# A decoder layer on one core: its first stage in pairs of token tiles

## What is computed

```
mod = silu(c) @ w_ada + b_ada                       # six rows of 1024: shift_a, scale_a, gate_a, ...
h   = rms_norm(x, g_attn) * (1 + scale_a) + shift_a # rms_norm: x * rsqrt(mean(x*x) + eps) * g
proj = h @ w_in                                     # queries, latents, index keys, keys, values
```

## Time and profile before

| | |
|---|---|
| median of 3 runs | 1016.02 us (1015.51 to 1017.2) |
| the profiled execution, its own time | 1018.29 us |
| its span in the profile | 1016.4 us |
| PE busy | 946.8 us, 93% of the span |
| DVE busy | 593.9 us, 58% |
| ACT busy | 401.1 us, 39% |
| POOL busy | 117.9 us, 12% |
| mean granted clock of PE, as a share of full speed | 0.971 |

### The profile page before, as it was taken

One profiled execution on the slowest core, in us unless ns is written; L12 is line 12 of the kernel. 1 busy time (PEld: TensorE's weight loads), 2 busy tenths in 40 slices (PEclk: granted clock), 3 DMA queues, 4 the chain that ended last, 5 costly groups with the idle time before them and its releaser, 6 DMA issues.

```text
span 1016.4 us, 14951 instructions
## 1 busy us (share of the span) xinstructions
PE 946.8 (93%) x5302; PEld 514.1 (51%) x5302; DVE 593.9 (58%) x1593; ACT 401.1 (39%) x909; POOL 117.9 (12%) x218
## 2 busy tenths in 40 slices
PE   3899999999999999999999999996699999979975
PEld 3464575444448756777766455554233433323421
DVE  2388647999999699987777234366222333212217
ACT  6131235666650488777668121212111221111113
POOL 3001000000008411110000000000111111111003
PEclk9999999999999899999999999998799999989988
DMA  9997100110111000040000421198799999999979
GB/s 325 331 358 266 42 22 23 41 42 23 41 42 27 1 1 2 1 182 9 1 2 1 186 83 63 66 368 325 278 404 421 420 420 420 419 422 420 394 291 373
DMA packets 70956, 191.96 MB, mean 189 GB/s; under 512 B 10264, under 2 KB 37200, under 8 KB 58592
## 3 DMA queue, kind: packets, MB, share of 16 engines
q1 hardware_dynamic: 62896, 173.15, 44.7%
q0 software_dynamic: 5760, 16.78, 4.2%
q10 hardware_dynamic: 2224, 1.05, 0.4%
HBM read 173.12 MB, written 22.04 MB: 192 GB/s over the span
## 4 chain that ended last, share of the span: by engine, by line
PE 65%; DVE 21%; DMA 6%; issue 5%; ACT 1%; POOL 1%; SPq 0%; POOLq 0%; DVEq 0%; ACTq 0%
PE PS L2006 12%; PE PS L1891 11%; DVE BIAS L1157 8%; PE PS L1784 6%; PE PS L2029 5%; PE PS L1827 5%; PE PS L1849 4%; DMA SC<-in_w_up_dram 3%; PE PS L1745 3%; PE PS L1697 3%; PE PS L1844 2%; DMA X<-residual_rows 2%; DVE X L1221 2%; PE PS L1993 2%; PE PS L1722 2%
## 5 line engine op out<-in xcount | busy, mean ns | idle before, releaser
L1697 PE MATMUL PS<-HT,X 128*128 128x512 f32 x384 | 168.8, 593 | 0.0
L2006 PE MATMUL PS<-QKV,HT 128*32 128x512 f32 (+2 forms) x640 | 131.2, 611 | 3.3 <-ACT HT L966 1.7
L870 ACT ACTIVATE X<-X,nmx 128x128 f32<-128x128 f32 (+7 forms) x128 | 98.4, 770 | 54.4 <-DVE nmx L1221 54.1
L1697 PEld LDWEIGHTS PS<-HT,X 128*128 128x128 f32 x384 | 72.5, 190 | 92.4 <-issue 92.4
L1891 PE MATMUL PS<-QKV,HT 128*128 128x512 f32 x256 | 113.7, 597 | 0.0
L1509 DVE TENSOR_TENSOR HT<-PS,HT 128x256 f32<-128x256 f32 x20 | 8.5, 424 | 153.7 <-ACT HT L974 153.7
L1157 DVE TENSOR_SCALAR_CACHE_REDUCE BIAS<-SC,tk 128x384 f32<-128x384 f32 (+3 forms) x128 | 96.4, 809 | 1.1
L853 ACT ACTIVATE X<-SC,tk 128x896 f32<-128x896 f32 x64 | 69.6, 1088 | 43.0 <-DVE tk L1145 43.0
L1784 PE MATMUL PS<-QKV 64*128 64x512 f32 (+3 forms) x384 | 81.3, 530 | 1.6 <-DVE nmx L1221 1.1
L1891 PEld LDWEIGHTS PS<-QKV,HT 128*128 128x128 f32 x256 | 47.4, 190 | 53.7 <-issue 53.6
L2029 PE MATMUL PS<-QKV,HT 128*32 128x512 f32 (+2 forms) x320 | 65.4, 595 | 1.8 <-DMA X<-in_w_down_dram 1.8
(11 more groups left out here) (296 smaller groups left out, 1489.3 us busy)
## 6 DMA issues: line engine op xcount, KB each, us to landing
QKV<-in_w_gate_dram SPq DMA_DIRECT2D x22, 1024.0 KB
QKV<-in_w_up_dram SPq DMA_DIRECT2D x22, 1024.0 KB
QKV<-in_w_down_dram SPq DMA_DIRECT2D x22, 1024.0 KB
QKV<-in_w_ada_dram SPq DMA_DIRECT2D x8, 2048.0 KB, 13.5
QKV<-in_w_ada_dram SPq DMA_DIRECT2D x8, 1024.0 KB, 12.5
X<-in_w_in_dram SPq DMA_DIRECT2D x16, 512.0 KB, 3.8
QKV<-expert_rows SPq DMA_DIRECT2D x16, 512.0 KB, 10.7
X<-in_w_gate_dram SPq DMA_DIRECT2D x5, 1024.0 KB
```

Source lines behind the costliest of these rows:

```text
L870: act.activation(sc, sc, ACT.Exp, bias=nmx[:, i % 4, m:m + 1], scale=-1.0, accum_out=rs[:, i, m:m + 1]).then_inc(exp_done, 1)
L1697: end = pe.matmul(PS[:, 2 * b + half, :], WS[:, b, j, :], HT[:, j, BANK * half:BANK * (half + 1)], start=(j == 0), stop=(j == KC - 1))
L2006: end = pe.matmul(PS[at, 2 + b, :], hgT[b][:, P * c_ + at.start:P * c_ + at.stop], WGU[w][:, c_, :, :], start=(c_ == 0), stop=(c_ == KC - 1))
```

## The change

It rewrites stage one for pairs of token tiles.

- ACT squares tiles 0, 2, 3, 4, 6 and 7; DVE squares tiles 1 and 5 itself (`square_x`, into a part of `HT` that is written again later). POOL forms 1/rms of two tiles at a time, waiting for both counts. DVE scales per pair.
- `turn_x` takes a pair and a list of feature blocks: two transposes per group and pair. The eight groups of the first half go to eight different PSUM banks, so none of them waits for a copy. The second half has four banks as before. DVE copies groups 0 and 1 as well.
- PE gets matmuls whose results nobody reads: nine of 128x512 ahead of the first transposes, and eight of 128x256 between the first pair and the second. They take the identity and the distance table `R`, and write to bank 7.
- The order on PE is new: pair 0, pair 1, pair 2 (blocks 0 to 3), `ada_part(0)`, pair 3 (blocks 0 to 3), `ada_cols(0)`, pairs 2 and 3 (blocks 4 to 7).
- On DVE the small folding work of the start now stands behind all of the scaling.

```diff
--- before.py
+++ after.py
@@ -321,15 +321,16 @@
         out_row_in, modc_set = sem("out_row_in"), sem("modc_set")
         wi_in, ws_in = sem("wi_in"), [sem(f"ws_in{i}") for i in range(2)]
         lam_ready, lam_exp, op_sb = sem("lam_ready"), sem("lam_exp"), sem("op_sb")
-        cols_ps, cols_sb, cexp_done, cact_done = sem("cols_ps"), sem("cols_sb"), sem("cexp_done"), sem("cact_done")
-        sq_done, rstd_done, xn_done = sem("sq_done"), sem("rstd_done"), sem("xn_done")
-        rstd_lat, rstd_x2, rstd_out = 3, 3, 3 + T
+        cols_ps, cols_sb, cact_done = sem("cols_ps"), sem("cols_sb"), sem("cact_done")
+        exp_sq_done, rstd_done, xn_done = sem("exp_sq_done"), sem("rstd_done"), sem("xn_done")
+        rstd_lat, rstd_x2, rstd_out = T // 2 + 1, T // 2 + 1, T // 2 + 1 + T
...
-        xt_on_dve = (9, 11, 13, 15)
-        xt_dve = sem("xt_dve")
+        xt_on_dve = (0, 1, 9, 11, 13, 15)
+        sq_on_dve = (1, 5)
+        xt_dve, sq_dve = sem("xt_dve"), sem("sq_dve")
         wcopy, fold_done = sem("wcopy"), sem("fold_done")
...
@@ -651,9 +652,10 @@
                 link(pool.tensor_scalar(ss[:, col:col + n], ss[:, col:col + n], 1.0 / width, EPS, ALU.mult, ALU.add))
                 return pool.tensor_tensor(ss[:, col:col + n], ss[:, col:col + n], neghalf[:, 0:n], ALU.pow)
 
-            for half in range(2):
-                pool.wait_ge(sq_done, T // 2 * (half + 1))
-                rstd(T // 2 * half, T // 2, D).then_inc(rstd_done, 1)
+            for t in range(0, T, 2):
+                pool.wait_ge(exp_sq_done, 1 + sum(a not in sq_on_dve for a in range(t + 2)))
+                pool.wait_ge(sq_dve, sum(a in sq_on_dve for a in range(t + 2)))
+                rstd(t, 2, D).then_inc(rstd_done, 1)
...
@@ -764,18 +766,18 @@
         @block.scalar
         def _(act):
             act.wait_ge(cols_sb, 1)
-            act.activation(cexp[:, :], cols[:, MODC:MODC + KC], ACT.Exp, scale=-1.0).then_inc(cexp_done, 1)
-            for t in range(T):
+            act.activation(cexp[:, :], cols[:, MODC:MODC + KC], ACT.Exp, scale=-1.0).then_inc(exp_sq_done, 1)
+            for n, t in enumerate(t for t in range(T) if t not in sq_on_dve):
                 act.wait_ge(x_in[t // 2], 16)
-                if t:
-                    act.wait_ge(sq_done, t)
-                act.activation(BIAS[:, 2, :], XT[:, t, :], ACT.Square, accum_out=ss[:, t:t + 1]).then_inc(sq_done, 1)
+                act.wait_ge(exp_sq_done, n + 1)
+                act.activation(BIAS[:, 2, :], XT[:, t, :], ACT.Square, accum_out=ss[:, t:t + 1]).then_inc(exp_sq_done, 1)
 
             for g in range(2 * KC):
                 half, j = g // KC, g % KC
                 if g not in xt_on_dve:
                     act.wait_ge(xt_ps, g + 1)
-                    act.activation(HT[:, j, BANK * half:BANK * (half + 1)], PS[:, g % 4, :], ACT.Copy).then_inc(xt_act, 1)
+                    act.activation(HT[:, j, BANK * half:BANK * (half + 1)], PS[:, g if g < KC else g % 4, :], ACT.Copy
+                                   ).then_inc(xt_act, 1)
...
@@ -1023,11 +1025,39 @@
             dve.tensor_copy(cols[:, :], PS[:, 6, 0:MODC + 2 * KC]).then_inc(cols_sb, 1)
 
             dve.wait_ge(cols_sb, 1)
-            dve.wait_ge(cexp_done, 1)
+            dve.wait_ge(exp_sq_done, 1)
             link(dve.tensor_scalar(cexp[:, :], cexp[:, :], 1.0, None, ALU.add))
...
+            def square_x(t):
+
+                dve.wait_ge(x_in[t // 2], 16)
+                dve.tensor_tensor_reduce(HT[:, KC - 1, :], XT[:, t, :], XT[:, t, :], 1.0, 0.0, ALU.mult, ALU.add,
+                                         ss[:, t:t + 1]).then_inc(sq_dve, 1)
+
+            def scale_x(t):
+
+                dve.wait_ge(rstd_done, t // 2 + 1)
+                dve.tensor_scalar(XT[:, t, :], XT[:, t, :], ss[:, t:t + 1], None, ALU.mult).then_inc(xn_done, 1)
+
+            def keep_x(g):
+
+                dve.wait_ge(xt_ps, g + 1)
+                bank = g if g < KC else g % 4
+                dve.tensor_copy(HT[:, g % KC, BANK * (g // KC):BANK * (g // KC + 1)], PS[:, bank, :]).then_inc(xt_dve, 1)
+
+            square_x(1)
+            for t in range(2):
+                scale_x(t)
+            dve.wait_ge(sq_dve, 1)
+            square_x(5)
+            for t in range(2, 6):
+                scale_x(t)
+            for g in xt_on_dve[:2]:
+                keep_x(g)
+            for t in range(6, T):
+                scale_x(t)
...
@@ -1038,10 +1068,6 @@
                                ).then_inc(dchain, 1)
             link.n += 2 * UNITS
             link(dve.tensor_scalar(cols[:, KC:2 * KC], cols[:, KC:2 * KC], 1.0, None, ALU.add))
-            for t in range(T):
-                dve.wait_ge(rstd_done, t // (T // 2) + 1)
-                dve.tensor_scalar(XT[:, t, :], XT[:, t, :], ss[:, t:t + 1], None, ALU.mult).then_inc(xn_done, 1)
-
...
@@ -1066,18 +1092,13 @@
                     dve.wait_ge(ada_done, i - 1)
                 dve.tensor_copy(halfsum[i % 2], PS[:, 4 + i % 2, :]).then_inc(part_sb, 1)
 
-            def keep_x(g):
-
-                dve.wait_ge(xt_ps, g + 1)
-                dve.tensor_copy(HT[:, g % KC, BANK * (g // KC):BANK * (g // KC + 1)], PS[:, g % 4, :]).then_inc(xt_dve, 1)
-
             for i in range(4):
                 if i == 0:
-                    for g in xt_on_dve[:2]:
+                    for g in xt_on_dve[2:4]:
                         keep_x(g)
                 keep_sums(i)
                 if i == 0:
-                    for g in xt_on_dve[2:]:
+                    for g in xt_on_dve[4:]:
                         keep_x(g)
                 a, b = slice(2 * i, 2 * i + 2), slice(KC + 2 * i, KC + 2 * i + 2)
                 dve.wait_ge(ada_done, i + 1)
@@ -1595,19 +1616,26 @@
             nv = MODC + 2 * KC
             pe.transpose(PS[:, 6, 0:nv], vrows, ident[0:nv, 0:nv]).then_inc(cols_ps, 1)
 
-            def turn_x(half, js):
-
-                pe.wait_ge(xn_done, 4 * half + 4)
+            def kept_x(g):
+
+                if g in xt_on_dve:
+                    pe.wait_ge(xt_dve, xt_on_dve.index(g) + 1)
+                else:
+                    pe.wait_ge(xt_act, g + 1 - sum(a < g for a in xt_on_dve))
+
+            def turn_x(pair, js):
+
+                half, i = pair // 2, 2 * (pair % 2)
+                pe.wait_ge(xn_done, 2 * pair + 2)
                 for j in js:
                     g = KC * half + j
-                    if g >= 4 and g - 4 in xt_on_dve:
-                        pe.wait_ge(xt_dve, xt_on_dve.index(g - 4) + 1)
-                    elif g >= 4:
-                        pe.wait_ge(xt_act, g - 3 - sum(a < g - 4 for a in xt_on_dve))
-                    for i in range(4):
-                        end = pe.transpose(PS[:, g % 4, P * i:P * (i + 1)], XT[:, 4 * half + i, P * j:P * (j + 1)],
-                                            ident[:, :])
-                    end.then_inc(xt_ps, 1)
+                    if half and i == 0:
+                        kept_x(j if j < 4 else KC + j - 4)
+                    for a in range(i, i + 2):
+                        end = pe.transpose(PS[:, g if g < KC else g % 4, P * a:P * (a + 1)],
+                                            XT[:, 4 * half + a, P * j:P * (j + 1)], ident[:, :])
+                    if i == 2:
+                        end.then_inc(xt_ps, 1)
 
             def ada_part(b):
 
@@ -1628,12 +1656,22 @@
                                      part32[:, :], start=True, stop=True)
                 end.then_inc(ada_done, 1)
 
+            for _ in range(9):
+                pe.matmul(PS[:, 7, :], ident[:, :], R[:, 0:BANK], start=True, stop=True)
+            pe.wait_ge(cols_sb, 1)
             turn_x(0, range(KC))
+            for _ in range(8):
+                pe.matmul(PS[:, 7, 2 * P:BANK], ident[:, :], R[:, 0:2 * P], start=True, stop=True)
+            turn_x(1, range(KC))
+            turn_x(2, range(4))
             pe.wait_ge(cact_done, 1)
+            kept_x(4)
             ada_part(0)
-            turn_x(1, range(4))
+            turn_x(3, range(4))
+            kept_x(7)
             ada_cols(0)
-            turn_x(1, range(4, KC))
+            turn_x(2, range(4, KC))
+            turn_x(3, range(4, KC))
 
             def ada_row(r):
 
```

## The result

Over 22 executions each, the changed kernel took 1018.06 us in the median (1015.63 to 1021.22) and the kernel before 1016.06 (1013.14 to 1018.96). The ratio is 1.0021, with a 95% interval of 1.0011 to 1.0030: slower by 2.1 us on the mean. Forecast was 1015.8, no change, and a range of 1013.5 to 1017.5.

What follows compares the result with a forecast made beforehand. PE's chain of waits through stage one was taken as the bound. ada_cols(0) comes 0.2 us earlier and the last transposes stay at low clock, so 1016.02 - 0.2 = 1015.8 us; range 1013.5 to 1017.5.

Steps and rivals of the forecast that it cites:

- Squares and power per pair: Start of stage one: first pair scaled at 11.1 us, 5.2 ahead of 16.28, but PE does not come to it; gain nothing.
- Nine unread matmuls: PE from 5.27 us: 7.94 us plus 2.4 for low clock, so real transposes start at 15.6 (14.9 to 16.5).
- Transposes, eight matmuls, `ada_part(0)`: PE up to group 11, without waits: 5.3, 3.5 and 1.85 us, sum 10.65, so group 11 at 26.25.
- Folding work behind the scaling: DVE, 23.9 to 25.6 us: takes 1.7 us, done before group 9 is there at 25.8, 0.2 to spare.
- the signs of being wrong: PE waits for copy or scaling; group 9's copy waits for folding; first projection moves without the program's end showing it.
- The detour to `ada_cols(0)`: From group 11 to ada_cols(0): 1.6 us instead of 1.37, so it starts at 27.85 against 28.07, a gain of 0.2.
- Last 16 transposes: PE behind ada_cols(0): 3.37 us if the clock falls again, total gain 0.2; 1.75 at 2.4 GHz, total gain 1.8.
- cases A to C: Clock behind ada_cols(0): A falls again, 1015.8 us, chance 0.53; B holds, 1014.2, 0.22; C low through projections, 0.10.
- rival C: Clock falls late and stays low through the first projections, 8 to 10 us: 1018.2 to 1019.2 us; chance 0.10.
- Rival D: Stage one: median run lacked a low stretch the profiled one had; unread matmuls hold PE back; 1016.7 us; chance 0.15.
- Behind stage one: After stage one: weight loads let 2.4 us of gain pass, DVE's modulation rows 3.6; a gain of 0.2 or 1.8 passes whole.
- Transposes and the clock: PE in stage one: transposes alone brought full clock back in the old trace; the skill's opposite rule would give 1017.5 us.

Runs made afterwards that it cites:

- the second profile: The changed kernel itself, nothing altered, run and profiled again on another chip; mean 1018.82 us, 2.5 (± 1.1) over the kernel before, ratio 1.0022.

## Why the prediction was wrong, point by point

- **Squares and power per pair: right.** First pair scaled at 10.7 (forecast 11.1), a custom square 1.23 us (1.22), and PE did not come to it.
- **Nine unread matmuls: right.** The transposes started between 14.8 and 16.1 us in the profiles of the kernels that have them; the forecast was 14.9 to 16.5. The spread follows the moment at which the granted clock rises: by what the 18 records take over 7.94 us, from 8.7 to 11.3 us after the start in these profiles.
- **Transposes, eight matmuls, `ada_part(0)`: right.** From 14.92 to 25.6, the end of group 11, is 10.7 us; forecast was 10.65.
- **Folding work behind the scaling: the step that failed.** It said "It spans 6.72 to 8.40 on DVE, 1.7 us", "covered, with 0.2 us to spare". The place was right to 1 us (it began at 22.91, forecast 23.9). The duration was carried from 7 us, where POOL does nothing, to 24 us, where POOL copies and sets, in the kernel before already:

```profile
24.08 1.04 POOL L658 COPY QKV<-QKV 128x1024 f32<-128x1024 f32 x1 [5.59 <-DMA QKV<-in_w_in_dram]
27.00 0.09 POOL L662 MEMSET tables<- 128x1 f32 x1
```

There the add took 0.26 to 1.79 us instead of 0.17. Where it came by 24.92 it was through by 25.2; where it came at 25.29 or 25.33 it stood until 27.0 or 27.1, and `ada_cols(0)` came 2.64 us behind the transposes instead of 1.64. That wait is 1.0 us; moving the folding work gives 2.0 us (± 1.2) back, and moving only POOL's memsets 1.6 (± 1.1). No group of rows showed POOL at 24 to 27 us: the row that mattered was not read. The chance that the spare time runs out was named, and given no size. That the copy of group 9 waits for the folding work stood among the signs of being wrong, and the second profile shows it.
- **The detour to `ada_cols(0)`: right where the folding work is out of the way** (1.64 us in its trace, forecast 1.6). It was 1.70 where the add ended in time, 2.64 in the changed kernel's second profile.
- **Last 16 transposes, cases A to C: the second step that failed.** The forecast let the low clock cost the 16 transposes 1.6 us and nothing more. It fell in both profiles of the changed kernel, but the transposes took 2.6 and 2.7 us instead of 3.4, and it reached through the first projection, to 36.0 and 37.7 us. In the first profile it cost 0.9 us in the transposes and 1.5 in the projection, in the second 1.0 and 1.4. Either sum is 0.7 us more than the 1.6 of before. It is rival C in mechanism, but at this size and not at 4 to 5 us. How it works on the mean is open: with both gaps filled, and the add still behind POOL, the mean lost nothing. That the first projection moves by a time that the end does not show was another sign, and the first profile has it: 1.5 us earlier, and the same end.
- **Rival D: its direction fits, and it is not shown.** The unread matmuls hold PE back in the traces. Without the eight (two kernels taken together), or with none, the mean stands 0.7 (± 0.9) and 1.0 (± 0.9) under the kernel before. The D given, +0.7, is about what is left in the kernel with the folding work first, 0.5 (± 1.0) over. Its premise, that the profile of the kernel before was a dear one, has something for it: its own time of 1018.29 lies 2.2 over the mean of that kernel. No second profile of it was taken, so this stays open.
- **Behind stage one: right up to 113 us.** The forecast ceiling of 2.4 us showed as starts of `ada_part(3)` at 43.2 to 43.4 in the kernels that came earlier, three of them with waits of 1.3 us for its weights, and what was gained or lost at `ada_part(1)` stood whole at the mark. The end of a single execution does not show it, for the low stretches behind.
- **Transposes and the clock.** The Trainium skill says that full clock does not engage for them ("TensorE: Matmul & The Clock Gate", "Part 4: PE-mode transpose"). No run here speaks for that. In the first run without unread matmuls PE had done only transposes, behind one small one at the start, when its clock rose between 14.7 and 15.5 us: the first 16 took 3.65 us, the next 16 took 1.97.

In sum: the add behind POOL's memsets is needed for the loss of 2 us, shown by moving either; it makes PE wait 1.0 us more, and the low clock that follows is the likely rest, since filling the gaps took the loss away as well. How the 2 us divide between wait and clock is not shown. What is left with the folding work first, 0.5 (± 1.0), has the direction and the size of unread matmuls that last longer than the wait they fill, and these executions do not tell it from nothing; the earlier first pair stays unused.

## What to carry to other kernels

A small operation that is moved on one engine must be priced where it lands, with what the other engines do there, not by its row from where it stood. Before moving DVE work, read POOL's timeline of the new place as well. Filler work on PE is free only up to the moment when its data arrives; measure it by that moment, and count anything beyond as delay. A loss that two different edits take away may need two conditions: run both edits together before giving one of them the whole sum. And where low stretches of the clock move the end of the program, compare traces at a mark close behind the change.

## What the runs showed of the hardware

- DVE's add on 128x8 in SBUF stood still through some sixty memsets of POOL in a row, 25.3 to 27.1 us. Each took 0.1, and one started every 0.03, so in the record they overlap and leave no moment free. In the same time DVE's copies out of PSUM ran at their usual 0.69 (the kernel before, 25.85 to 27.4). The Trainium skill has a mechanism ("SBUF — State Buffer", "Who interferes with whom"): VectorE and GpSimd share one pair of ports, and when a VectorE operation runs in a mode that uses that pair, whoever comes second is blocked for the whole instruction. The traces agree, and show that such a row of short ones blocks like one long one. That the add runs in such a mode no run shows.
- Not all of DVE's work stands behind POOL: in the changed kernel's second profile its eight memsets ran from 24.37 to 25.26 in their usual 0.89 us, while POOL copied.
- It goes the other way too. In the changed kernel POOL's power on two columns took 1.71 us, from 12.29 on, while DVE squared a tile (12.21 to 13.4), and 0.72 with DVE idle.
